# A three-block transformer kernel: the first block's early modulation summed by VectorE, its projection in halves

## The reference, cut

```
mod = c @ w_ada + b_ada                                   # six vectors of 1024
sh1, sc1, gt1, sh2, sc2, gt2 = split(mod, 6)
h = rms_norm(x, g_mix) * (1 + sc1) + sh1
p = h @ w_in + b_in
q, k, v, o, gates, hx = split(p)
y_m = mlstm_mixer(q, k, v, o, gates, ...)                 # forward + backward, per-head rms norm, sigmoid(o) gate
y_h = hyena_mixer(hx, ...)                                # short conv, two long convs by FFT, group rms norm
x = x + gt1 * (concat([y_m, y_h]) @ w_out)
hf = rms_norm(x, g_ffn) * (1 + sc2) + sh2
x = x + gt2 * expert_choice_moe(hf, w_router, w_gate, w_up, w_down)    # 16 experts
```

## Time and profile before

| | us |
|---|---|
| timed runs, median (lowest, highest) of 3 | 2254.64 (2252.96, 2260.94) |
| the profiled execution | 2251.38 |
| its span | 2249.6 |
| TensorE busy in it | 2001.7 |
| VectorE, ScalarE, GpSimd busy | 577.2, 417.4, 191.5 |
| DMA | 664.24 MB, mean 295 GB/s |

### The profile page before, as it was taken

How to read it: one execution, slowest core, us unless ns; L and a number is a source line. 1 busy time by engine, 2 the same in 40 slices (tenths; PEclk the granted TensorE clock), 3 DMA queues, 4 the chain that set the end, 5 groups by cost and what they waited for, 6 DMA issues and landing times.

```text
span 2249.6 us, 32668 instructions
## 1 busy us (share of the span) xinstructions
PE 2001.7 (89%) x14156; PEld 1403.0 (62%) x14156; DVE 577.2 (26%) x1183; ACT 417.4 (19%) x766; POOL 191.5 (9%) x183
## 2 busy tenths in 40 slices
PE   6999988886788888987888887999999999999997
PEld 3865665542455556653555543756888877588886
DVE  5168221104421100000001101454432034630001
ACT  2122121201310100000000211434200033630001
POOL 0520000002000000000000000235000003600000
PEclk9999989998999999999999989999999999999999
DMA  9558899999999999999999999531487842044450
GB/s 364 209 200 331 329 422 423 399 426 424 411 392 426 427 425 424 422 422 426 424 424 425 424 374 413 141 113 38 171 297 218 192 141 88 27 150 150 126 154 19
DMA packets 181287, 664.24 MB, mean 295 GB/s; under 512 B 17336, under 2 KB 121305, under 8 KB 142553
## 3 DMA queue, kind: packets, MB, share of 16 engines
q1 hardware_dynamic: 181144, 662.15, 75.2%
HBM read 661.08 MB, written 1.05 MB: 294 GB/s over the span
## 4 chain that ended last, share of the span: by engine, by line
PE 47%; DMA 21%; DVE 4%; ACT 3%; issue 1%; POOL 0%; SPq 0%; ACTq 0%; DVEq 0%; POOLq 0%
PE ps L1148 19%; PE ps L650 10%; DMA ring<-in_context_weights 8%; DMA ring<-in_w_gate 6%; DMA ring<-in_w_down_slots 5%; PE ps L1532 4%; DMA ring<-in_w_up 2%; PE ps L1558 2%; PE ps L984 2%; PE ps L1157 2%; PE ps L951 2%; ACT arena L2427 1%; PE ps L846 1%; PE ps L676 1%; PE ps L812 1%
## 5 line engine op out<-in xcount | busy, mean ns | idle before, releaser
L1148 PE MATMUL ps<-arena,ring 128*128 128x256 f32 x1984 | 429.9, 379 | 1.4 <-DVEq L389 1.4
L1148 PEld LDWEIGHTS ps<-arena,ring 128*128 128x128 f32 x1984 | 376.5, 190 | 54.6 <-DVEq L389 1.9
L1532 PE MATMUL ps<-ring,arena 128*32 128x256 f32 x4032 | 259.3, 403 | 83.7 <-DMA ring<-in_w_gate 44.4
L650 PE MATMUL ps<-arena,ring 128*128 128x256 f32 (+2 forms) x1372 | 309.5, 385 | 8.9 <-DMA ring<-in_context_weights 7.3
L650 PEld LDWEIGHTS ps<-arena,ring 128*128 128x128 f32 (+2 forms) x1372 | 249.2, 187 | 74.6 <-DMA ring<-in_context_weights 24.6
L1532 PEld LDWEIGHTS ps<-ring,arena 128*32 128x32 f32 x4032 | 126.0, 114 | 202.2 <-DMA ring<-in_w_gate 53.6
L2134 ACT ACTIVATE arena<-ps 128x512 f32<-128x512 f32 (+3 forms) x143 | 76.6, 536 | 742.8 <-PE ps L650 333.2
L1558 PE MATMUL ps<-ring,arena 128*32 128x512 f32 x1024 | 143.7, 692 | 54.1 <-DMA ring<-in_w_down_slots 47.3
L1558 PEld LDWEIGHTS ps<-ring,arena 128*32 128x32 f32 x1024 | 30.8, 120 | 148.6 <-DMA ring<-in_w_down_slots 81.5
L1236 PE MATMUL ps<-arena,ring 128*128 128x256 f32 x512 | 112.0, 380 | 1.0 <-DMA ring<-in_w_out 1.0
L2939 POOL TENSOR_TENSOR XC<-XC,arena 128x256 f32<-128x256 f32 x32 | 23.3, 729 | 989.9 <-ACT XC L2228 969.6
(11 more groups left out here) (358 smaller groups left out, 1921.0 us busy)
## 6 DMA issues: line engine op xcount, KB each, us to landing
ring<-in_w_up SPq DMA_DIRECT2D x64, 2048.0 KB, 13.5
ring<-in_w_down_slots SPq DMA_DIRECT2D x64, 2048.0 KB, 14.1
ring<-in_w_gate SPq DMA_DIRECT2D x62, 2048.0 KB, 13.4
ring<-in_w_ada SPq DMA_DIRECT2D x36, 2048.0 KB, 9.6
ring<-in_w_ffn_in SPq DMA_DIRECT2D x44, 1024.0 KB, 7.5
ring<-in_context_weights SPq DMA_DIRECT2D x35, 1024.0 KB, 14.1
ring<-in_w_ffn_out SPq DMA_DIRECT2D x16, 1408.0 KB, 7.0
ring<-in_w_in SPq DMA_DIRECT2D x9, 2048.0 KB, 8.0
```

The lines of the kernel that those rows point to most:

```text
L650: m = mm(o, a, x, start=(k == 0 and r == 0), stop=(k == kt - 1 and last))
L1148: m = mm(b, w[:, k, c:c + P], src[:, k, :], start=(k == 0), stop=(k == kt - 1))
L1532: m = mm(b[u][32 * c:32 * c + 32, T * x:T * x + T], xs[:, 2 * h + k, CAP * e:CAP * e + CAP], w[:, k, at_:at_ + T], start=(h == 0 and k == ...
```

## The change

1. **Rows.** Slots ada4 to ada9 leave the stream. Their bytes come as twelve transfers of 1 MB, "modulation rows" (128x2048; `load_row`), into three dead buffers in turn. SP issues them behind x2 (rows 0 to 5), v (6 to 8), ada10 (9, 10) and ada11 (11); the first waits for the filter spectra, each later one for the sum of the row that used its buffer. VectorE multiplies each by a column of c and adds it up (`rows_added`): eight rows in `sums1`, four in `sums2`, nine of them ahead of the gates, three behind q's convolution. TensorE sums `sums1` over partitions with 4 matmuls (`ada_sum`, half a slot's); `sums2` opens the bank that ada10 and ada11 go on with.
2. **Order.** z is the fifth slot. ada10 and ada11 follow v, ada0_0 to ada0_2 follow o, ada0_3 to ada0_6 follow k; nine slots are behind out1, with ada0_9 and ada0_10 in dead parts of `arena` (they wait for the second spectrum product and for the last numerators). The steps are a list of groups (`ADA`), with a turn behind the first slot of the next group.
3. **Hyena norms as columns.** ScalarE squares z; TensorE forms 8 columns (4 wide, bank `hss`); root and reciprocal work on 128x8; 8 transposes (`hsb`) spread them.
4. **Numerators.** All of one direction first, denominators of a direction in one 128x8 piece (`DN`, `norms`); the forward h goes through ScalarE, the backward one through VectorE, head by head.
5. **Projection in halves** (`out_half`): the hyena half of mix0, mix1 ahead of the heads' transposes, that of mix2, mix3 behind them, then both mLSTM halves.
6. ScalarE takes the router's exponential ahead of h's copies; VectorE begins the selection after one bank.

```diff
-        stream = [(f"ada{j}", ada_slot(w_ada, j)) for j in range(5)]
-        at_tile = 5
-        for n, count in (("z", 0), ("x1", 0), ("q", 1), ("x2", 1), ("v", 1), ("o", 1), ("k", 11)):
+        stream, at_tile = ada_tiles[:4], 10
+        for n, count in (("z", 0), ("x1", 0), ("q", 0), ("x2", 0), ("v", 2), ("o", 3), ("k", 4)):
...
+        row_buffer = [i % 3 for i in range(9)] + [0, 1, 0]
+        def row_place(i):
+            return at((0, 2048, 16424)[row_buffer[i]], 2048)
...
+        early |= {n: {"ada0_9": 5120, "ada0_10": 0}[name] for n, (name, _) in enumerate(stream) if name in ("ada0_9", "ada0_10")}
...
+            def ada_sum(name, g):
+                pe.wait_ge(late_used, (0, 8, SUMMED)[g])
+                row_bank[0] = open_bank(pe, f"row_{name}{g}", ADA_BANKS)
+                for x in range(4):
+                    m = mm(row_bank[0][32 * x:32 * x + 32, :], ones[:, 0:32], (sums1, sums2)[g - 1][:, 2 * x:2 * x + 2, :], start=True, stop=(g == 1))
...
+            def out_half(j, heads):
+                ks = range(4, 8) if heads == "hyena" else range(4)
...
+            pe.wait_ge(yh_ready, 2)
+            out_half(0, "hyena")
             pe.wait_ge(hn_ready, 1)
...
+            out_half(1, "hyena")
             pe.wait_ge(ym_ready, 1)
             for j in range(2):
-                w = take(f"out{j}")
+                out_half(j, "mlstm")
                 release_with(f"mix{2 * j + 1}")
...
+            def rows_added(first, last):
+                for i in range(first, last):
+                    total, k = (sums1, sums2)[i // 8], i % 8
+                    dve.wait_ge(*row_landed(i))
+                    w = row_place(i).rearrange("p (a b) -> p a b", b=T)
+                    if k == 0:
+                        step(ts(total, w, pc("c", k), None, ALU.mult), late_used)
+                    else:
+                        step(stt(out=total, in0=w, scalar=pc("c", k), in1=total, op0=ALU.mult, op1=ALU.add), late_used)
+            step(v.memset(vtok, 1.0))
+            rows_added(0, 9)
             dve.wait_ge(s_row, 64)
...
             qk_conv(0)
-            ada()
+            rows_added(9, SUMMED)
...
+            def load_row(i):
+                if i == 0:
+                    read_bank(sp, "kim11")
+                if row_before(i) is not None:
+                    sp.wait_ge(late_used, row_before(i) + 1)
+                sp.dma_start(row_place(i), modulation_row(i)).then_inc(row_landed(i)[0], 16)
+            rows_behind = {"x2": range(6), "v": range(6, 9), "ada10": range(9, 11), "ada11": range(11, 12)}
```

More of the change, by code:

```diff
@@ L602, in stage_of, with ada_steps @@
             return row_stage[:, (GROUP[name] + j) % 2, :]
-        def ada_steps(tiles, rows, turn):
+        def ada_steps(rows, turn, summed):
             at_step = [0]
@@ L1443, in _ @@
                         close_bank(m, f"num{d}{t}{hp}")
-                ada()
-            ada(3)
+            pe.wait_ge(p_ready, 1)
+            numerators(0)
+            pe.wait_ge(yh_ready, 1)
+            for c in range(2):
+                b = open_bank(pe, f"hsb{c}", MIX_BANKS)
+                for i in range(4):
+                    j = 4 * c + i
+                    m = nc.tensor.transpose(b[:, P * i:P * i + P], hyr[:, j:j + 1].to_broadcast([P, P]), ident)
+                close_bank(m, f"hsb{c}")
+            numerators(1)
+            wo = [None, None]
+            def out_half(j, heads):
+                if heads == "hyena":
+                    wo[j] = take(f"out{j}")
+                ks = range(4, 8) if heads == "hyena" else range(4)
+                for i in range(2):
+                    name = f"mix{2 * j + i}"
+                    b = open_bank(pe, name, MIX_BANKS) if heads == "hyena" else ps[place[name][0]]
+                    for x in range(2):
+                        for k in ks:
+                            src = yT[:, k, :] if k < 4 else hxc[:, 4 + k, :]
+                            c = P * (2 * i + x)
+                            m = mm(b[:, T * x:T * x + T], wo[j][:, k, c:c + P], src, start=(k == 4 and x == 0), stop=(k == 3 and x == 1))
+                    if heads == "mlstm":
+                        close_bank(m, name)
+            pe.wait_ge(yh_ready, 2)
+            out_half(0, "hyena")
             pe.wait_ge(hn_ready, 1)
@@ L2020, in dve_mixers @@
             tell(yh_ready)
-            ada(3)
-            dve.wait_ge(ss_ready, 1)
+            norms(1)
+            for t in range(TT):
+                for hp in range(2):
+                    name = f"num1{t}{hp}"
+                    b = read_bank(dve, name)
+                    for i in range(2):
+                        j = H * t + 2 * hp + i
+                        dve.wait_ge(ss_ready, j + 1)
+                        step(stt(out=hs[:, j, :], in0=b[:, 129 * i:129 * i + P], scalar=DN[:, 1, j:j + 1], in1=hs[:, j, :],
+                                 op0=ALU.mult, op1=ALU.add), hs_ready, frees=name if i else None)
+                        if i:
+                            tell(hs_ready)
```

232 lines of the change are left out of this document (130 added, 102 removed).

## The result

The changed kernel takes **2265.9 us** (median of 20 runs, 2261.2 to 2270.8) where the kernel before takes 2255.7 (20 runs on the same chip, 2251.5 to 2261.6). The ratio is **1.0043**, interval 1.0034 to 1.0053: slower by 10 us, where the forecast was 11 faster and the range ended at 2255. The profiled executions are further apart, spans of 2264.6 against 2249.6: the profiled one of before lies 4 us under its median, that of after on it. (In the table of the experiments, two of the twelve runs of no. 8 took 5,270 and 5,711 us and are left out.)

A forecast was written before the change was run, and what follows sets the result against it. The experts' stage was taken as bound by DMA, its start by the ring's gating in the first block. The output projection ending 12.1 us earlier, less a 1.2 us longer tail, gave 10.9: 2244 us, range 2236 to 2255.

The forecast's parts named there:

- E: End of the output projection in the first block: 259.2 before, forecast at 247.1, 12.1 us earlier.
- the tail: From the output projection's end to the context input's landing: 33.2 us instead of 32.0, so 1.2 us longer.
- Step 1: Start of z: its weights take ada4's place in the stream, so z starts at 49.2, gain 3.5 us.
- Step 3: Modulation rows ahead of the gates: 2.8 us each back to back, rows 0 to 8 done at 89.9.
- Step 4: Up to the token rows: they start at 113.6 instead of 113.9, almost all that was won given back.
- Step 5: From token rows to the first inverse transform: 25.8 us, to 139.4, with VectorE's chain just covered.
- Step 8: Numerators to the output projection's end: the first hyena half, 7.0 us, covers the heads' norm; end at 247.1.
- The rule weighed: VectorE and GpSimd's shared port locked for whole instructions: rows 0 to 8 would end 2 us later, gain 9.
- Rows for nothing: Rival on the modulation rows: VectorE and GpSimd don't meet, token rows at 110.7, gain 13.8, 2241 us; chance 0.27.
- GpSimd starved: Rival on the modulation rows: long row operations make GpSimd's z late, priced at 7 us, gain 4, 2251; chance 0.14.
- It does not reach the end: Rival on the experts' stage or the tail: held elsewhere or by slots, gain about 0, 2255 us; chance 0.07.
- slower: Rival on the row loop: rows don't overlap, at 6 us a row gain -12, 2267 us; chance 0.06.

The follow-up runs named there:

- no. 8: no. 4 with slot ada0_11 used ahead of the router's product, not behind the transposes of h; 2248.5 us, ratio 0.9966.
- no. 6: no. 4 with both hyena halves of the output projection behind the heads' transposes again; 2255.5 us, ratio 1.0002.
- no. 5: Changed kernel with both waits removed, VectorE adding only 8 of 2048 columns of each modulation row, transfers kept; 2250.6 us, ratio 0.9975.
- no. 4: Changed kernel with both waits removed, and rows 7 and 8 added behind the gates; 2243.6 and 2244.6 us, ratios 0.9952 and 0.9949.

## Why the prediction was wrong, step by step

It went wrong by 26 us between profiles (10.9 faster forecast, 15.0 slower profiled), of which E is 15.7, the tail 4.9, the stream's blocks 4.8 and the experts' stage 0.5.

- **Step 1** held in this profile: z at 49.15 (49.2), behind a wait of 3.3. It isn't the rule. Of the twelve profiles of kernels with the change, six have z at 48.6 to 49.2 and six at 52.2 to 53.4; in the first six the filter network's run of 64x512 matmuls, ahead of it, took 7.1 to 7.8 us, in the others 14.0. The three profiles of kernels without the change have 52.7 to 53.6 either way. So the 3.5 us of this step are there in six of the twelve profiles, and a single profile can be off by 4 us.
- **Step 2** held: the summed group at 92.40, over at 93.5 (93.4).
- **Step 3** was off by 1 us. F at 96.04 (94.9). The row was costed too high, its arrival too early: back to back 2.57 us (2.8 taken, 2.35 alone), but the first sum began at 64.0 (62.2), VectorE waited 5.2 us for the row behind v's slot, and the rows were over at 91.6 (89.9).
- **Step 4** was off by 4.2: token rows at 117.77 (113.6). VectorE had the gates' columns at 115.0, 1.4 late; the rest is the clock at 0.50, which lengthened F, the turn, z by token and x2. The sum took the durations of the kernel before, all at clock 1.00, though it put a wait in front of them. GpSimd's z, over at 95.7 (97.0), held nobody.
- **Step 5 is the step that failed first and most.** 25.8 us were forecast from token rows to the first inverse transform and 36.4 measured: 7.8 for the bank, 2.9 for the clock behind it, both of which the sum had at nothing. The moved turn was counted as 1.05 us of TensorE (step 4) and 0.2 of VectorE, and step 5 asked whether VectorE's chain was covered, by its data. It didn't ask which bank the moved turn holds and what VectorE does before it gives it back. Half of the answer, free3 on the turn, stands among the rows of the change ahead of the prediction; the other half, free3 on the spectrum's first product, is in the same instruction order.
- **Step 6** held: 55.2 us between the transforms (55.5).
- **Step 7** held: 15.7 (15.6), with a wait of 3.25 where 4 was forecast.
- **Step 8** held as a mechanism: no wait for the heads' norm longer than 0.3, and no. 6 shows 7.1 if the halves are gone. From the numerators to E it was 37.7 (36.6); the numerators' 24 matmuls took 4.59 instead of 2.95, at a granted clock of 0.66 in that window.
- **The tail** failed in one term, from the last scaling to the router's product: 5.5 us forecast and 11.4 measured. The last scaling ends at E + 11.0 as forecast, the copy 0.8 later. But the tile of ada0_8 too comes only behind the copy (3.64), and then a turn of 1.88 (1.05) and two tiles of 5.26 (3.84): the router's product at E + 22.4 (E + 16.5). A tile takes 1.92 at the full clock; the granted clock was 0.50 from 274 to 282, so some 4 of these 5.9 us are the clock behind the 6.4 us wait, and 1.9 the tile. From there it was shorter than forecast (5.2 for 6.6). Issue to landing was 10.1, as forecast. The term that the sum lacked altogether is the 4.8 us behind the experts: the gain was carried unchanged to the end.
- **The rule weighed.** GpSimd's operations beside a row took up to 2.84 us, where they take 0.55 to 0.92 alone, one of them per row; the row pays 0.2 us on average (timelines of VectorE and of GpSimd):

```profile
66.50 12.87 DVE L1965 SCALAR_TENSOR_TENSOR XC<-arena,par,XC 128x2048 f32<-128x2048 f32 x5 [1.20 <-DMA arena<-in_w_ada]
```

```profile
66.83 2.62 POOL L3023 TENSOR_TENSOR arena<-arena 128x256 f32<-128x256 f32 x1
69.54 2.84 POOL L3022 TENSOR_SCALAR arena<-arena,par 128x256 f32<-128x256 f32 x1
```

A lock held for a whole instruction, as the Trainium skill has it ("SBUF — State Buffer", section "Who interferes with whom"), fits GpSimd's side: it waits out the rest of a row. For VectorE the price is below both values that I weighed.
- **The rivals.** None was it. "Rows for nothing" is right in that the sums cost nothing (no. 5), wrong in that the two engines don't meet, and wrong in its time: F waits even without the sums. "GpSimd starved" fell with GpSimd's z at 95.7, before the forecast's 97.0. "It does not reach the end" fell too: what was lost when the input landed (9.7) is there at the last products (10.2). Of "slower" I had only mechanisms of the rows. The range ended 11 us under the result, since it held no case in which a moved instruction takes a shared bank, and none in which the stream's length matters.

With both waits removed the plan gives 2249 and 2247, with the rows behind the gates 2244. That is the time that was forecast, in part by luck: in its two profiles E is at 251.6 and 248.3 (247.1), the context input lands 28.0 and 28.4 after it (33.2), thanks to the early copy, and the stream's stops, which the forecast lacked, are in it. With the stream shifted back it is **2238.9, 0.9928 (0.9914 to 0.9942)**, faster than both kernels and the best version found.

## What to carry to other kernels

When an instruction that opens a bank or a buffer is moved, look for the one that gives it back, on the engine that drains it, and count everything that stands before that in its program; the data dependence is only half of the wait. Price every term behind a new wait of TensorE at the lower clock too. Where a kernel has long runs of tiny matmuls, the number of instructions ahead of them is a parameter of its own: compare the waits marked "issue" before and after an edit, and try a shift of some tens of instructions. And before two single profiles are subtracted, compare their starts: here z's alone differed by 4 us between executions.

## What the hardware showed that I had not expected

- Stops of 1.0 to 2.6 us in runs of 32x32 matmuls, at fixed instruction numbers, 194 modulo 256 by the count above, each ending 1.2 to 1.6 us after an instruction transfer of 16.4 KB. Not every border stops TensorE in every version: at instruction 19,906 the changed kernel stopped for 1.01 us, and no. 4 in neither of its profiles. The two long stops come where the border before lies in the same dense run, which suggests that the speed at which a block is used up decides; no run varies it.
- The clock of one and the same program falls in one execution and not in the next: 0.50 from 100 to 105 in no. 4's first profile, 1.00 in its second, with 16.49 and 14.06 us for the same 64 matmuls. In the fifteen profiles it falls nine times around this half of x2, each time with a wait of TensorE of 0.54 to 4.03 us between the second half of q and x2. The five profiles without such a wait keep 1.00, and so does no. 8, with a wait of 0.51. What decides between a fall and none after such a short wait stays open.
- GpSimd's 256-column operations stretched threefold beside 2048-column ones of VectorE, while these lost under a tenth.
